# A six-block transformer on one core: plain transposes moved earlier, compression in four column tiles, one convolution tile on GpSimd

## What is computed

```python
# convolution: 512 channels, 31 taps, causal
u = a * jax.nn.sigmoid(b)
u = lax.conv_general_dilated(u, conv_w[:, None, :], ..., feature_group_count=CONV_CH) + conv_b
u = jax.nn.silu(layernorm(u, ln_g, ln_b)) ; return u @ w_proj
# compression, once for keys and once for values: 15 blocks x 2 groups, each of 32 tokens x 64
blk = tok[:, idx] + pos[:, None, :]
blk = blk.transpose(0, 1, 3, 2, 4).reshape(bsz, n_cmp, NSA_KV_GROUPS, CMP_BLOCK * NSA_HEAD_DIM)   # 2048 long
return jax.nn.gelu(blk @ w1 + b1) @ w2                                                           # w1: 2048 x 256
```

## Time and profile before

| | us |
|---|---|
| median of 3 runs | 3058.84 (3057.62 to 3064.43) |
| the profiled execution, device time | 3060.01 |
| its span, first to last instruction | 3058.3 |
| PE busy | 3012.4 |
| DVE busy | 1851.5 |
| ACT busy | 1478.5 |
| POOL busy | 84.4 |

### The profile page before, as it was taken

How to read it: one execution, slowest core, us unless ns; L and a number is a source line. 1 busy time by engine, 2 the same in 40 slices (tenths; PEclk the granted TensorE clock), 3 DMA queues, 4 the chain that set the end, 5 groups by cost and what they waited for, 6 DMA issues and landing times.

```text
span 3058.3 us, 38507 instructions
## 1 busy us (share of the span) xinstructions
PE 3012.4 (99%) x15611; PEld 2561.8 (84%) x15611; DVE 1851.5 (61%) x2319; ACT 1478.5 (48%) x2159; POOL 84.4 (3%) x153
## 2 busy tenths in 40 slices
PE   8999999999999999999999999999999999999999
PEld 6889888888888889788888988898888889888887
DVE  5556655546655546754555665578775547877554
ACT  5445544435544435644544554444655434465542
POOL 0000000000000001100000000010000001000000
PEclk9999999999999999999999999999999999999999
DMA  6563555555555555255556445574244557524453
GB/s 227 191 209 131 172 181 193 184 192 194 186 185 192 180 192 186 90 193 187 191 182 209 154 158 180 191 216 158 77 166 151 184 184 219 168 81 166 152 183 134
DMA packets 302403, 532.99 MB, mean 174 GB/s; under 512 B 31074, under 2 KB 125204, under 8 KB 302228
## 3 DMA queue, kind: packets, MB, share of 16 engines
q1 hardware_dynamic: 288964, 511.63, 51.1%
q10 hardware_dynamic: 13264, 18.90, 1.8%
HBM read 528.33 MB, written 1.11 MB: 173 GB/s over the span
## 4 chain that ended last, share of the span: by engine, by line
PE 94%; DVE 3%; ACT 1%; DMA 1%; issue 1%; POOL 0%; ACTq 0%; SPq 0%; POOLq 0%; DVEq 0%
PE bank L722 90%; PE bank L1008 2%; PE bank L1036 1%; DVE sb_parts L1790 1%; DMA sb_ring<-in_w_xq_dram 1%; ACT sb_hT_high L1270 1%; DVE sb_sc L1971 0%; ACT sb_parts L1296 0%; PE bank L782 0%; PE bank L774 0%; ACT sb_sc L1432 0%; DVE sb_prT L1981 0%; DMA sb_ring<-in_ff_w_in_dram 0%; PE bank L799 0%; DMA sb_arena<-in_norm_ffn_dram 0%
## 5 line engine op out<-in xcount | busy, mean ns | idle before, releaser
L1790 DVE TENSOR_TENSOR sb_parts<-sb_ring,sb_parts 128x2048 fp32r<-128x2048 f32 x480 | 1098.3, 2292 | 802.8 <-ACT sb_parts L1296 800.8
L722 PE MATMUL bank<-sb_parts,sb_hT_high 128*128 128x512 f32 (+1 forms) x4480 | 1378.5, 394 | 8.4 <-DVE sb_parts L1790 5.2
L1296 ACT ACTIVATE sb_parts<-sb_ring 128x2048 fp32r<-128x2048 f32 x480 | 914.9, 1913 | 793.8 <-PE bank L722 695.8
L722 PEld LDWEIGHTS bank<-sb_parts,sb_hT_high 128*128 128x128 f32 x4480 | 839.6, 189 | 186.9 <-issue 11.6
L722 PE MATMUL bank<-sb_parts,sb_hT_low 128*128 128x512 f32 (+1 forms) x2240 | 855.6, 392 | 0.0
L722 PE MATMUL bank<-sb_parts,sb_hidden_high 128*128 128x512 f32 x1760 | 545.9, 391 | 0.0
L722 PEld LDWEIGHTS bank<-sb_parts,sb_hT_low 128*128 128x128 f32 x2240 | 423.9, 189 | 89.3
L722 PEld LDWEIGHTS bank<-sb_parts,sb_hidden_high 128*128 128x128 f32 x1760 | 329.7, 188 | 73.1 <-issue 0.6
L722 PE MATMUL bank<-sb_parts,sb_hidden_low 128*128 128x512 f32 x880 | 345.5, 393 | 0.0
L722 PE MATMUL bank<-sb_hT_high,sb_parts 128*128 128x256 f32 x1408 | 254.5, 283 | 0.0
L722 PEld LDWEIGHTS bank<-sb_hT_high,sb_parts 128*128 128x128 f32 x1408 | 220.1, 192 | 0.2
(11 more groups left out here) (215 smaller groups left out, 2164.3 us busy)
## 6 DMA issues: line engine op xcount, KB each, us to landing
sb_ring<-in_ff_w_in_dram SPq DMA_DIRECT2D x160, 1024.0 KB, 5.2
sb_ring<-in_ff_w_out_dram SPq DMA_DIRECT2D x88, 1024.0 KB, 4.9
sb_ring<-in_w_gate_up_dram SPq DMA_DIRECT2D x40, 1024.0 KB, 5.2
sb_ring<-in_w_in_dram SPq DMA_DIRECT2D x38, 1024.0 KB, 5.1
sb_ring<-in_a_w_qkv_dram SPq DMA_DIRECT2D x24, 1024.0 KB, 5.2
sb_ring<-in_w_down_dram SPq DMA_DIRECT2D x22, 1024.0 KB, 5.0
sb_ring<-in_ff_w_in_dram SPq DMA_DIRECT2D x32, 512.0 KB, 4.9
sb_ring<-in_c_w_qkv_dram SPq DMA_DIRECT2D x12, 1024.0 KB, 5.1
```

The lines of the kernel that those rows point to most:

```text
L722: return nc.tensor.matmul(o, lhsT, rhs, start=start, stop=stop)
L1296: nc.scalar.activation(halves(n, slice(0, filled(n))).high, ring[:, raw_in[n], 0:filled(n)], ACT.Copy) \
L1790: V.tensor_tensor(both.low, ring[:, raw_in[n], 0:filled(n)], both.high.bitcast(F32), ALU.subtract) \
```

## The change

Three edits: (1) the transposes of tile 0 of the next plain norm are issued in the stage before, ahead of its last product step of three matmuls (in `memory` ahead of its last two matmuls), and those of tile 1 ahead of the last two matmuls of tile 0; (2) compression makes `blk` stationary (32 columns, padded with zeros) and the 256 hidden units moving, in four groups of 32 output partitions; ACT copies the four partial sums to SBUF, and two more matmuls per v, after the gate product, add them up with a 0/1 matrix `fold` and turn them; the gelu stands behind the sigmoids; (3) channel tile 3 of the convolution is computed by POOL, a multiplication and an addition per tap.

```diff
+        fold = sb("fold", [P, 2, CMP_STRIDE])
-        blk = flat[:, 4 * S:4 * S + 960].rearrange("p (v j g c) -> p v j g c", v=2, j=16, g=2)
+        blk = flat[:, 4 * S:8 * S].rearrange("p (v j g c) -> p v j g c", v=2, j=16, g=2)
+        hid_sums = tmp[:, :].rearrange("p (v n) -> p v n", v=2)
...
-            def pair_mm(o, src, weights, b, first, last, high, low):
+            def pair_mm(o, src, weights, b, first, last, high, low, between=None):
...
+                if between:
+                    between()
                 pe.wait_ge(dve_sig.sem, dve_sig.at(dve_key))
                 for k in pair:
                     ins = mm(o, src(k).low, weights(k).high, False, last and k == pair[1])
...
+                    if between and n == len(pairs) - 1:
+                        between()
                     one = split_mm if type(lhsT) is Split else mm
...
+            def next_tile(st):
+
+                follows = norm_after(st)
+                if follows and follows != "final" and in_rows(follows[0]):
+                    return lambda: norm_tile(follows[0], 0)
+
             def first_rows(st, ckeys, key):
 
                 n = (st, "norm")
-                for t in range(NT):
-                    norm_tile(st, t)
+                early = in_rows(st) and st != stages[0]
+                for t in range(NT):
+                    if not early:
+                        norm_tile(st, t)
...
-                                          b == 0, b == 3, (act_step, (n, t, b)), (dve_read, (n, t, b)))
+                                          b == 0, b == 3, (act_step, (n, t, b)), (dve_read, (n, t, b)),
+                                          (lambda: norm_tile(st, 1)) if early and (t, b) == (0, 3) else None)
...
-                            512, bank=banks[t][1])
+                            512, bank=banks[t][1], between=next_tile(st) if t == NT - 1 else None)
...
+                                    if (t, h, n, kk) == (NT - 1, 1, together + 1, 1) and next_tile(key[0]):
+                                        next_tile(key[0])()
                                     ins = part_of(t, h, n, kk)
...
-                        hid_banks = [YB.take(pe, (st, "hid", v, f)) for f in range(2)]
+                        hid_bank = YB.take(pe, (st, "hid sums", v))
...
                         wv = raw_view((*L, "cmp", v, h))
+                        for j in range(8):
+                            r = 32 * (j % 4)
+                            ins = mm(hid_bank[r:r + 32, 0:CMP_HIDDEN], blk[:, v, 8 * h + j, :, :].rearrange("p g c -> p (g c)"),
+                                     wv[:, j, :], h == 0 and j < 4, h == 1 and j >= 4)
+                        key = (st, "hid sums", v) if h else (st, "hid half", v)
+                        ins.then_inc(matmul_done.sem, matmul_done.next(key))
+                        chunk_end[(*L, "cmp", v, h)] = key
+
+                    rows_gemm([(*L, "merge", c, h) for h in range(2)], (st, "merge", c), hT, banks, compress if banks else None)
+                    if banks:
+                        hid_bank = YB.take(pe, (st, "hid", v))
+                        pe.wait_ge(dve_step.sem, dve_step.at("fold"))
+                        pe.wait_ge(act_read.sem, act_read.at((st, "hid sums", v)))
                         for f in range(2):
-                            for j in range(8):
-                                ins = mm(hid_banks[f][:, 0:30], wv[:, j, f * P:(f + 1) * P],
-                                         blk[:, v, 8 * h + j, :, :].rearrange("p g c -> p (g c)"), h == 0 and j == 0, h == 1 and j == 7)
...
+                            ins = mm(hid_bank[:, f * 2 * N_CMP:(f + 1) * 2 * N_CMP], hid_sums[:, v, f * P:(f + 1) * P],
+                                     fold[:, :, 0:N_CMP], True, True)
...
                 pe.wait_ge(dve_step.sem, dve_step.at((st, "conv")))
+                pe.wait_ge(pool_step.sem, pool_step.at((st, "conv", CT - 1)))
...
+                        copy(hid_sums[:, v, :], G.of((st, "hid sums", v))[:, 0:CMP_HIDDEN]) \
+                            .then_inc(act_read.sem, act_read.next((st, "hid sums", v)))
                     for t in range(NT):
                         act.wait_ge(matmul_done.sem, matmul_done.at(((st, "merge", c), t)))
...
+                    if c in (1, 2):
+                        act.wait_ge(matmul_done.sem, matmul_done.at((st, "hid", v)))
+                        for f in range(2):
+                            ins = nc.scalar.activation(hid_c[:, v, f, :], G.of((st, "hid", v))[:, f * 2 * N_CMP:(f + 1) * 2 * N_CMP],
+                                                       ACT.Gelu_apprx_tanh, bias=gcol((("cmp_b1_k_2", "cmp_b1_v_2")[v], l), f))
...
                     power((st, "latent"), 4, 4)
+                    c = CT - 1
+                    pool.wait_ge(dve_step.sem, dve_step.at((st, "glu")))
+                    for tap in range(TAPS):
+                        wt = convwT[:, i, tap * CT + c:tap * CT + c + 1]
+                        src = glu[:, c, tap:tap + S]
+                        if tap == 0:
+                            ins = pool.tensor_scalar(convT[:, c, :], src, wt, gcol(("conv_b_2", i), c), ALU.mult, ALU.add)
+                        else:
+                            weighed_tap = prT[:, 1, (tap % 2) * S:(tap % 2 + 1) * S]
+                            step(pool.tensor_scalar(weighed_tap, src, wt, None, ALU.mult), (st, "tap", tap))
+                            ins = pool.tensor_tensor(convT[:, c, :], convT[:, c, :], weighed_tap, ALU.add)
+                        ins.then_inc(pool_step.sem, pool_step.next((st, "conv", c)))
                     power((st, "conv"), 4, 2)
...
+                step(V.memset(blk[:, :, :, :, N_CMP:CMP_STRIDE].rearrange("p v j g c -> p (v j g) c"), 0.0))
...
-                        for c in range(CT):
+                        for c in range(CT - 1):
...
+                step(V.tensor_reduce(fold[:, :, :], ident[:, :].rearrange("p (n g c) -> p g c n", n=4, g=2), AX.X, ALU.add), "fold")
```

More of the change, by code:

```diff
@@ L745, in _, with product @@
             awaited = []
-            def product(key, pairs, width, rows=P, c0=0, bank=None, done=True):
+            def product(key, pairs, width, rows=P, c0=0, bank=None, done=True, between=None):
                 o = (G.take(pe, key) if bank is None else bank)[0:rows, c0:c0 + width]
@@ L1124, in compress @@
                         wv = raw_view((*L, "cmp", v, h))
-                        for f in range(2):
-                            for j in range(8):
-                                ins = mm(hid_banks[f][:, 0:30], wv[:, j, f * P:(f + 1) * P],
-                                         blk[:, v, 8 * h + j, :, :].rearrange("p g c -> p (g c)"), h == 0 and j == 0, h == 1 and j == 7)
-                            key = (st, "hid", v, f) if h else (st, "hid half", v, f)
-                            ins.then_inc(matmul_done.sem, matmul_done.next(key))
+                        for j in range(8):
[4 more added lines that the diff above has]
+                        ins.then_inc(matmul_done.sem, matmul_done.next(key))
                         chunk_end[(*L, "cmp", v, h)] = key
                     rows_gemm([(*L, "merge", c, h) for h in range(2)], (st, "merge", c), hT, banks, compress if banks else None)
+                    if banks:
[5 more added lines that the diff above has]
+                                     fold[:, :, 0:N_CMP], True, True)
+                        ins.then_inc(matmul_done.sem, matmul_done.next((st, "hid", v)))
                     if c == 3:
                         pe.wait_ge(small_loaded.sem, small_loaded.at(st))
-                        pe.wait_ge(act_read.sem, act_read.at((st, "hid", 1, 1)))
+                        pe.wait_ge(act_read.sem, act_read.at((st, "hid", 1)))
                         product((st, "kc"), [(w2k[:, f, :, :].rearrange("p u d -> p (u d)"), hid_c[:, 0, f, :]) for f in range(2)], 30,
@@ L1235, in memory @@
                                           lambda k: view(ckeys[k // 2])[:, k % 2, h * 512:(h + 1) * 512], b, b == 0, b == 1,
-                                          (act_step, n), (dve_read, n))
+                                          (act_step, n), (dve_read, n), next_tile(st) if (t, h, b) == (1, 1, 1) else None)
                         ins.then_inc(matmul_done.sem, matmul_done.next(((st, "y"), t, h)))
@@ L1564, in branches @@
                         v = c - 1
[L1565 to L1569, removed]
+                        act.wait_ge(matmul_done.sem, matmul_done.at((st, "hid sums", v)))
+                        copy(hid_sums[:, v, :], G.of((st, "hid sums", v))[:, 0:CMP_HIDDEN]) \
+                            .then_inc(act_read.sem, act_read.next((st, "hid sums", v)))
                     for t in range(NT):
@@ L1573, in branches @@
                             .then_inc(act_read.sem, act_read.next(((st, "merge", c), t)))
+                    if c in (1, 2):
+                        act.wait_ge(matmul_done.sem, matmul_done.at((st, "hid", v)))
```

(8 more changed lines are left out.)

## The result

The changed kernel takes **3064.71 us** (median of 21 runs, 3058.76 to 3068.49); the kernel before takes 3060.0 beside it. The ratio is **1.0014**, 95% interval 1.0007 to 1.0020: 0.14% slower, just outside its own interval, inside the 0.2% that the prediction called no change. 3050, a gain, was forecast. The range 3022 to 3070 held it.

A forecast was written before the change was run, and what follows sets the result against it. PE, busy for 99% of the span, was taken as the bound, with DVE next in the compression stage. 3060.0 - 5.9 (transposes) - 2.8 (compression and convolution) = 3051.3, less 1.2 to the median: 3050 us, range 3022 to 3070.

The forecast's parts named there:

- the one reduction for `fold`: In the compression: this reduction goes to an engine that waits at that point and was priced at nothing.
- B: Rival: POOL holds DVE longer at the low parts of m10 to m21; 1.15 us a tap makes 3071; chance 0.25.
- Early transposes: At the norm boundaries: matmuls behind the transposes cover a 0.31 us wait for ACT's copy, 19 x 0.31 = 5.9 us.
- Compression on PE: In each `l2` layer: a compression half takes 0.92 us instead of 3.49, if the four column tiles run at once.
- rival C: Compression: column tiles run one by one and POOL's holds are at their lower end, 3042 us; chance 0.08.
- PE's 32.6 us: Compression stretch of both layers: PE's own need falls by 17.9 + 14.7 us; nearly 30 go into waits for low parts.
- The convolution: POOL's taps block DVE for 0.75 us each: 22.8 us of holds a layer against 12.5 us freed.
- low parts "well over" 2.29 us: Sign of being right: low parts on DVE run well over 2.29 us while POOL works.
- Which wait ends last: From glu product to the convolution's rows: PE waits for low parts and arrives at 93.7 us, a gain of 2.8.
- the 34.96 us follow: Stretch behind the compression, up to the convolution's rows: takes 34.96 us as before, after the fold at 58.7.
- No fall of the clock behind a `compress` half: Sign of being right: PE's clock does not fall behind a compression half of about 0.9 us.
- A: Rival: DVE is not held up by POOL, so PE's need decides: 3020 us, or 3022 with loading limits; chance 0.17.

The follow-up runs named there:

- run 1: The changed kernel with the 128 bytes of `fold` allocated behind `arena` instead of in front of it: 3052.02 us, ratio 0.9976 to the kernel before.
- run 2: The kernel before with an unused tile of 128 bytes where the change puts `fold`: 3070.51 us, ratio 1.0038.
- run 8: The kernel before with the early transposes alone: 3051.04 us, ratio 0.9978.
- run 7: The kernel of run 5 with all eight compression matmuls of a half in one column tile: 3048.96 us, ratio 0.9969 to the kernel before.
- run 9: The kernel before with the compression in column tiles alone, `fold` behind `arena`, the convolution all on DVE: 3038.16 us, ratio 0.9931.
- run 5: The changed kernel with `fold` behind `arena` and the convolution's fourth channel tile back on DVE: 3030.58 us, ratio 0.9911 to the kernel before.
- run 6: The kernel of run 1 with POOL's taps replaced by clears, leaving out the fourth channel tile: 3025.96 us, ratio 0.9897 to the kernel before.

## Why the prediction was wrong, and where it was right

**The step that failed** is the sentence that prices "the one reduction for `fold`" at nothing, in the part on the compression. The reduction costs nothing; the tile's place costs 11.6 us, and the sum has no term for where things lie. 3051.3 + 11.6 = 3062.9, and the profiled execution took 3063.6. Runs 1 and 2 show the term from both sides, 0.38% each. The sign of the result hangs on it alone. That the range of 3022 to 3070 held the result is luck: its upper part was there for B, longer holds by POOL, and the holds came out shorter.

**Early transposes: right.** 5.9 forecast, 6.7 (4 to 9) measured in run 8. The place at the second mixer, counted as nothing, lost about 0.9 us (1.31 of wait against 0.26 and 0.15).

**Compression on PE: right.** A half takes 1.0 us (0.92 forecast) and the tiles overlap; rival C falls with run 7. Of PE's 32.6 us the kernel keeps 21 where DVE does the whole convolution (run 9).

**The convolution: right in mechanism, the sum nearly.** DVE and POOL take turns. The Trainium skill (SBUF — State Buffer, Who interferes with whom) has a DVE instruction with two SBUF inputs contend with a GpSimd instruction that reads SBUF, and not with one that only writes it. The trace agrees with both: 13.26 us for 21 taps beside POOL's taps, 8.42 beside its clears. The hold of a POOL tap is 0.68 us, not 0.75. By the Trainium skill's figure (GPSIMD Engine Reference, Elementwise — side-by-side cycle accounting) it would have been 0.25 + 0.56 = 0.81, so the trace is below that estimate. Two details were wrong. POOL was slower to come back than assumed: a turn every one and a half taps, not after each. And low parts "well over" 2.29 us, named as a sign of being right, did not come: they kept their 2.28. POOL's last addition was taken up 79.5 us after the glu product and ended at 85.8, while the nine DVE taps beside it came 0.40 us apart; why POOL got no turn there is not shown.

**Which wait ends last: right total by luck, two errors that cancel.** PE reached the rows at 93.6 and 92.3 (93.7 forecast). But the low part of m10 was ready at 21.7, not 24.2, and the next ones 7.8 apart, not 9.55; the fold of m21 was done at 51.2 and 51.9, not 58.7. And "the 34.96 us follow" is wrong: 42.36 and 40.43 followed, 4.34 and 3.62 of it the wait for DVE's copies behind `merge` 4, nearly all the rest the clock (0.92 and 0.96, before 1.00). "No fall of the clock behind a `compress` half" was named as a sign of being right too, and in layer 1 it fell behind the first half and the wait that followed (0.90). A DVE that is behind is paid for again wherever PE needs something from its list. I followed only the low parts and the sum of the taps.

**The rivals.** A (no hold-up) is what the kernel does once POOL is off the SBUF reads: 3026 to 3031 in runs 5 and 6, 3022 forecast. B put the slower end in POOL's holds; slower came about, but from no rival of mine.

## What to carry to other kernels

Before costing a change, list what it allocates and which later tiles move by that; where PE is the bound, a shift of a stationary operand by 128 bytes can outweigh a reordering of the work (11.6 us against 6.7 here). A part whose cost is covered must be costed again beside every other part that shortens the cover, and every item on a late engine's list must be followed, not only the dearest. DVE work given to POOL is paid back in DVE's time where both read SBUF as here, 0.68 us of hold for 0.40 us saved.

## What the runs showed of the hardware

- The pitch of 128x512 float32r matmuls depends on the difference of the two operands' SBUF addresses over 256 bytes: 227.0 ns at 0, 229.4 at 192, 233 to 234 at the other multiples of 32. Why is not shown.
- POOL's multiplications and additions, which read SBUF, hold up DVE instructions with two SBUF inputs (21 DVE taps in 13.3 us); 128x256 clears every 0.31 us did not (8.4 us). A DVE instruction of 2048 columns kept its 2.28 us, and POOL's record beside it grew to 3.22.
- Four column tiles of 32 take a group of eight 128x256 float32 matmuls from 3.57 to 1.00 us.
- The clock also fell in or behind waits of 3 to 4 us: 4.34 us behind `merge` 4 of layer 0 (0.92 in that stretch, where it had been 1.00), 3.24 us ahead of m10 in layer 1 (0.90). It did not each time: 3.21 us ahead of m10 in layer 0 left it at 1.00.
